# Two-block network on one core: late queries and U products moved between the spread batches, and the ranking of gathered heads moved by up to two dense steps

## What is computed

```
q = (hb @ w_q).reshape(C, PEER_HEADS, 2, PEER_DK_HALF)
s = einsum('thpd,hpnd->thpn', q, sub_keys)
sv, si = top_k(s, 16)
cand = sv[:, :, 0, :, None] + sv[:, :, 1, None, :]
fv, fpos = top_k(cand.reshape(C, PEER_HEADS, 256), 16)
g = softmax(fv)
a = gelu(einsum('ted,td->te', u_tab[eidx], hb))
y = einsum('te,ted->td', g * a, v_tab[eidx])
```

## Time and profile before

| | us |
|---|---|
| median of 3 runs (lowest, highest) | 2140.14 (2136.9, 2140.8) |
| the profiled execution's own time | 2128.76 |
| its span, first to last instruction | 2126.6 |
| TensorE busy | 2001.9 (94%) |
| VectorE busy | 1474.8 (69%) |
| GpSimd busy | 1064.6 (50%) |
| ScalarE busy | 454.8 (21%) |
| DMA bytes moved | 529.21 MB |

### The profile page before, as it was taken

One profiled execution on the slowest core, in us unless ns is written; L12 is line 12 of the kernel. 1 busy time (PEld: TensorE's weight loads), 2 busy tenths in 40 slices (PEclk: granted clock), 3 DMA queues, 4 the chain that ended last, 5 costly groups with the idle time before them and its releaser, 6 DMA issues.

```text
span 2126.6 us, 27946 instructions
## 1 busy us (share of the span) xinstructions
PE 2001.9 (94%) x10152; PEld 1490.0 (70%) x10152; DVE 1474.8 (69%) x3128; ACT 454.8 (21%) x916; POOL 1064.6 (50%) x905
## 2 busy tenths in 40 slices
PE   7999999999999998899988999999999999999796
PEld 6888866878898865678876666666666666666563
DVE  3673034333553596747997998989989898978668
ACT  4122223133453315522222010100101010010000
POOL 4354432427203743222534866675766757566562
PEclk9999999999999999999988999999999999999998
DMA  9565423524101312014447999999999999999996
GB/s 246 164 227 187 137 70 129 196 79 131 51 3 53 119 33 90 1 60 145 133 157 277 413 414 414 413 413 414 413 413 414 413 413 414 413 413 412 399 414 255
DMA packets 130070, 529.21 MB, mean 249 GB/s; under 512 B 14208, under 2 KB 18736, under 8 KB 113200
## 3 DMA queue, kind: packets, MB, share of 16 engines
q0 software_dynamic: 73728, 268.47, 31.8%
...
...
## 4 chain that ended last, share of the span: by engine, by line
PE 42%; DMA 29%; DVE 19%; POOL 4%; issue 4%; ACT 2%; SPq 0%; DVEq 0%; ACTq 0%; POOLq 0%
PE ps L782 26%; DMA work<-in_peer_v,consts 10%; DMA work<-in_peer_u,consts 7%; DMA ring<-in_peer_v,consts 6%; DMA ring<-in_peer_u,consts 6%; PE ps L1099 3%; PE ps L1111 2%; PE ps L868 2%; POOL ring L2377 1%; POOL work L2377 1%; PE ps L810 1%; PE ps L924 1%; DVE ring L1848 1%; DVE tables L1894 1%; DVE work L1894 1%
## 5 line engine op out<-in xcount | busy, mean ns | idle before, releaser
L1111 PE MATMUL ps<-work,tmp 128*128 128x512 f32 x1024 | 463.2, 606 | 22.9 <-DVE tmp L1914 22.9
L2298 POOL TENSOR_TENSOR w_lo<-ring,w_hi 128x1024 fp32r<-128x1024 f32 (+2 forms) x116 | 274.6, 2374 | 394.9 <-ACT w_hi L1969 394.8
L1099 PE MATMUL ps<-hT,work 128*128 128x256 f32 x2048 | 453.0, 379 | 0.0
L1099 PEld LDWEIGHTS ps<-hT,work 128*128 128x128 f32 x2048 | 388.8, 190 | 79.1 <-issue 29.6
L1111 PEld LDWEIGHTS ps<-work,tmp 128*128 128x128 f32 x1024 | 193.3, 193 | 246.3 <-issue 223.2
L2377 POOL DMA_INDIRECT ring<-in_peer_u,consts x136 | 174.1, 1280 | 118.2 <-DVE hT L1870 35.7
L2377 POOL DMA_INDIRECT ring<-in_peer_v,consts x138 | 165.4, 1199 | 104.1 <-DVE tables L1894 45.6
L782 PE MATMUL ps<-w_hi,x_hi 128*128 128x512 f32 (+2 forms) x544 | 208.2, 383 | 1.1 <-DVE tmp L1437 1.1
L782 PE MATMUL ps<-w_lo,x_hi 128*128 128x512 f32 (+2 forms) x544 | 207.2, 381 | 0.0
L1969 ACT ACTIVATE w_hi<-ring 128x1024 fp32r<-128x1024 f32 (+2 forms) x116 | 120.4, 1042 | 392.3 <-PE ps L782 287.2
L2377 POOL DMA_INDIRECT work<-in_peer_v,consts x118 | 149.6, 1268 | 84.9 <-DVE tables L1894 38.5
...
## 6 DMA issues: line engine op xcount, KB each, us to landing
work<-in_u_steps SPq DMA_DIRECT2D x64, 1024.0 KB, 8.0
work<-in_peer_v SPq DMA_DIRECT2D x64, 1024.0 KB
...
```

Of the source, the lines that this page charges most:

```text
L1099: mm = pe.matmul(ps[:, 4 + s, j * DT:(j + 1) * DT], u_ring[:, s, j, k, :], hT[:, k, GATHERED * P:T], start=(k == 0), stop=(k == KD - 1))
L1111: mm = pe.matmul(ps[:, 2 * t + half, :], tmp[:, s, j * DT + t * P:j * DT + (t + 1) * P], v_ring[:, s, j, half * BANK:(half + 1) * BANK], s ...
L2298: pool.tensor_tensor(w_lo[q % NPIECE][:, 0:n], ring[:, at:at + n], w_hi[q % NPIECE][:, 0:n], ALU.subtract).then_inc(w_split, 1)
```

## The change

Query 12 moves ahead of the spread batches: its first half between the second and the third transposed table, its second half behind the third. Queries 13 to 15 then fill batches m = 0 to 5, and the U products of dense steps 0 and 1 fill m = 6 to 13, a quarter of a step's product (one j, four of eight k) behind each batch. The third table moves to bank 1. In the ranking, the reduce (L1778) moves from piece 6 to piece 7, and the pieces of a head move: those of head 1 stand in dense steps 0 to 5, those of head 2 and later begin at s = 6 of the head before the last, so that piece 6 stands in s = 3, a U step, and piece 7 in s = 5.

```diff
--- before.py
+++ after.py
@@ -55,6 +55,8 @@
 BLOCK = SLOTS * 2 * GATHERED // STEPS
 HEAD_SLOTS = GATHERED * TOPK
 U_STEPS = HEAD_SLOTS // BLOCK
+FIRST_PIECES = ((0,), (1, 2), (3, 4), (5,), (6,), (7,))
+NEXT_PIECES = ((0,), (1,), (2, 3), (4,), (5,), (6,), (), (7,))
 EPS = 1e-6
 LAMBDA_INIT = 0.8 - 0.6
 NEG = -1.0e30
@@ -93,7 +95,7 @@
 ADA_LAG = 2
 ATT_LAG = 4
 LATE_FIRST = 12
-U_FIRST = 2 * (2 * PEER_H - LATE_FIRST)
+U_FIRST = 2 * (2 * PEER_H - LATE_FIRST - 1)
 ATT_SLOTS = 8
 C_CHUNKS = {0: Q_LAT, 1: KV_LAT + ROPE, 2: BANK, 3: BANK, 4: BANK}
 
@@ -232,11 +234,13 @@
         jobs.add("pqL", f)
         if f >= 1:
             jobs.add("peer_l", f - 1)
-    for i, b in enumerate((4, 5, 1)):
-        jobs.put(b, "pairs", i)
+    for i in range(2):
+        jobs.put(4 + i, "pairs", i)
     for f in range(LATE_FIRST, 2 * PEER_H + 1):
         if f < 2 * PEER_H:
             jobs.put(f % 2, "pqL", f)
+        if f == LATE_FIRST:
+            jobs.put((f + 1) % 2, "pairs", 2)
         jobs.put(2 + f % 2, "peer_l", f - 1)
     return jobs, units
 
@@ -1071,15 +1075,24 @@
                 if f >= 1:
                     key_scores("pqL", "peer_l", f - 1, f - 1)
 
-            pe.wait_ge(picked, 2 * PEER_H - 1)
-            for i in range(3):
-                pe.wait_ge(routed, 3 if i == 2 else 2)
+            def table(i, src):
+
                 o = start("pairs", i)
-                src = r_sel[:, i, :, :, :] if i < 2 else r_g
                 for t in range(DENSE):
                     mm = pe.transpose(o[:, t * P:(t + 1) * P],
                                       src[:, t, :, :].rearrange("p h k -> p (h k)"), ident[:])
                 end(mm, "pairs", i)
+
+            pe.sem_inc(spread_summed, 2)
+            pe.wait_ge(picked, 2 * PEER_H - 1)
+            pe.wait_ge(routed, 2)
+            for i in range(2):
+                table(i, r_sel[:, i, :, :, :])
+            query("pqL", "pql", LATE_FIRST, LATE, ALL[0:KD // 2])
+            pe.wait_ge(routed, 3)
+            table(2, r_g)
+            query("pqL", "pql", LATE_FIRST, LATE, ALL[KD // 2:])
+            key_scores("pqL", "peer_l", LATE_FIRST - 1, LATE_FIRST - 1)
 
             def spread_gates(m, s):
 
@@ -1091,14 +1104,14 @@
                                        hot_j[s][part][:, t // TWIN, :, t % TWIN], start=(part == 0), stop=(part == PARTS - 1))
                 mm.then_inc(spread_summed, 1)
 
-            def dense_u(s, load, js=range(PAIR)):
+            def dense_u(s, load, js=range(PAIR), ks=range(KD)):
 
                 pe.wait_ge(u_loaded[s], load)
                 for j in js:
-                    for k in range(KD):
+                    for k in ks:
                         mm = pe.matmul(ps[:, 4 + s, j * DT:(j + 1) * DT], u_ring[:, s, j, k, :],
                                        hT[:, k, GATHERED * P:T], start=(k == 0), stop=(k == KD - 1))
-                if js[-1] == PAIR - 1:
+                if js[-1] == PAIR - 1 and ks[-1] == KD - 1:
                     mm.then_inc(u_done, 1)
 
             def dense_v(n, s, load, first=False, last=False):
@@ -1117,19 +1130,18 @@
 
             for b in range(4, NB):
                 pe.wait_ge(bank_free[b], jobs.uses[b])
-            pe.sem_inc(spread_summed, 2)
             for m in range(RSTEPS):
                 spread_gates(m, m % 2)
-                f, half = LATE_FIRST + m // 2, m % 2
-                if f < 2 * PEER_H:
+                f, half = LATE_FIRST + 1 + m // 2, m % 2
+                if m < U_FIRST:
                     query("pqL", "pql", f, LATE, ALL[half * 4:half * 4 + 4])
                     if half == 1:
                         key_scores("pqL", "peer_l", f - 1, f - 1)
-                elif m < U_FIRST + 2 * PAIR:
+                elif m < U_FIRST + 4 * PAIR:
                     if m == U_FIRST:
                         key_scores("pqL", "peer_l", f - 1, f - 1)
-                    n, j = divmod(m - U_FIRST, PAIR)
-                    dense_u(n, 16, range(j, j + 1))
+                    n, j = divmod((m - U_FIRST) // 2, PAIR)
+                    dense_u(n, 16, range(j, j + 1), ALL[half * 4:half * 4 + 4])
             for b in range(4):
                 pe.wait_ge(bank_free[b], jobs.uses[b])
             for n in range(2):
@@ -1772,11 +1784,11 @@
                         eq = late[h].eq[a].rearrange("p (t k) a -> p t k a", k=TOPK)
                         late_steps(dve.tensor_tensor(eq, eq, r.idxf[:, a].unsqueeze(2).to_broadcast([P, n, TOPK, TOPK]),
                                                      ALU.mult))
+                else:
                     late_steps.settle()
                     for a in range(2):
                         eq = late[h].eq[a].rearrange("p (t k) a -> p t k a", k=TOPK)
                         late_steps(dve.tensor_reduce(late[h].sel[:, a], eq, AX.X, ALU.add))
-                else:
                     late_steps.settle()
                     late_steps(dve.scalar_tensor_tensor(eidx[:, h], late[h].sel[:, 0], float(NKEYS), late[h].sel[:, 1],
                                                         ALU.mult, ALU.add))
@@ -1916,10 +1928,12 @@
                     one_hots(region + 1, n + RSTEPS)
                 if s == U_STEPS:
                     head_coefs(h)
-                if h + 1 < PEER_H and s < 7:
-                    late_piece(h + 1, s)
-                    if s == 6:
-                        late_piece(h + 1, 7)
+                if n < len(FIRST_PIECES):
+                    for piece in FIRST_PIECES[n]:
+                        late_piece(1, piece)
+                elif (n + 2) // HEAD_STEPS + 1 < PEER_H:
+                    for piece in NEXT_PIECES[(n + 2) % HEAD_STEPS]:
+                        late_piece((n + 2) // HEAD_STEPS + 1, piece)
                 if s < U_STEPS:
                     gather_u(h, s)
                 else:
@@ -2195,7 +2209,7 @@
                 taken(act.activation(d_h2[:, i // 2, (i % 2) * BANK:(i % 2 + 1) * BANK], o, ACT.Copy), "h2", i)
             act.wait_ge(x_kept, 16 * NT)
             act.wait_ge(xn_done, NT * 4)
-            for f in range(LATE_FIRST):
+            for f in range(LATE_FIRST + 1):
                 if f == LATE_FIRST - 2:
                     normalise_gates()
                 keep_query("pqL", "peer_l", f)
@@ -2219,8 +2233,8 @@
             act.sem_inc(spread_kept, 2)
             for m in range(RSTEPS):
                 keep_gates(0, m)
-                f = LATE_FIRST + m // 2
-                if m % 2 == 1 and f < 2 * PEER_H:
+                f = LATE_FIRST + 1 + m // 2
+                if m % 2 == 1 and m < U_FIRST:
                     keep_query("pqL", "peer_l", f)
                     keep_late(f - 1)
                 if m == U_FIRST:
```

## The result

| | before | after |
|---|---|---|
| median, 5 runs each side by side | 2137.70 us | 2127.82 us |
| lowest to highest | 2135.91 to 2140.80 | 2123.18 to 2129.84 |
| profiled execution | 2128.76 | 2129.84 |
| its span | 2126.6 | 2128.0 |

The ratio of the times is 0.9948, with a 95% interval of 0.9930 to 0.9965: the changed kernel is faster by 0.35 to 0.70%, 7.5 to 15 us; the medians are 9.9 us apart. The forecast was 8.6 us less, 2131.5 us.

A forecast was written before the change was run, and what follows sets the result against it. The DMA stream was taken to bound the dense steps, its restart hanging on the spread batches' end. The loop's 8.6 us (4.1 plus 4.5), with ranking 0, off the 2140.1 us median gave 2131.5; own range 2129 to 2134, wider 2127 to 2137.5.

The forecast's parts named there:

- the saving is the same there: Whole kernel: the profiled execution's saving of 8.6 us also holds for the median of 2140.1 us, giving 2131.5.
- I take 0: Ranking pieces moved among the dense steps: no change in the end time, between -3 and +3 us.
- What bounds the kernel: Dense steps are bound by DMA at 413 GB/s; the spread batches' end sets the restart, and 8.6 us passes on whole.
- Query 12 moved ahead: Before batch 0: two halves of 1.82 us and 0.44 of scores fit TensorE's waits, cost nothing; the loop loses 4.1 us.
- The 4.5 left for the waits: Spread loop: VectorE's late-batch waits and the slow clock at batch 4 hold the remaining 4.5 us of the saving.
- Batches 0 to 5: Spread loop's start: VectorE stays last, first gather stays at 1102, 1.3 to 1.4 us lost at batch 4 is saved.
- Batches 6 to 15: Rest of the spread loop: 2.57 us a batch on TensorE, sixteenth batch kept near 1129.9 us, 8.6 us sooner.
- The profiled execution at 2120.2 us: Whole kernel: the profiled execution falls from 2128.8 us by 8.6 to 2120.2.
- rival (b): Dense steps: the ranking helps as well, the stream loses 2 to 3 us less, 2128 to 2129.5 us; 12%.
- Rival (c): Dense steps: slower, GpSimd's gather issue becomes the bound from 1.6 us an issue on, 14 us given back, 2145; 5%.
- Rival (d): Spread loop: half the gain, TensorE falls to the low clock again or batch 15 waits, 2134 to 2137 us; 10%.

The follow-up runs named there:

- a_again: The changed kernel run again unaltered on chip 0, beside the kernel before: ratio to before 0.9959, median 2125.97 us.
- spread_only: The changed kernel with the old ranking and the reduces of L1778 back in piece 6, on chip 0: ratio to the kernel before 0.9974, 2128.09 us.
- a_third: The changed kernel run once more unaltered on chip 11, beside the kernel before: ratio to before 0.9945, median 2126.70 us.
- s_third: The changed kernel with the ranking as before, on chip 11: ratio to the kernel before 0.9970, median 2131.48 us.
- early8: The changed kernel with all eight gathered rows of the first U step reduced before the wait for step 0's gelu, chip 11: ratio to before 0.9962, 2131.45 us.
- delay: The changed kernel with the U product of dense step 1 computed twice more behind batch 10, chip 15: ratio to the kernel before 1.0025, 2136.09 us.
- late_gathers: The changed kernel with the first gather held until the sixteenth batch's tables are written, chip 15: ratio to the kernel before 1.0004, 2131.71 us.
- rank_only: The kernel before with only the ranking pieces and the reduces of L1778 moved, chip 0: ratio to before 1.0002, median 2136.76 us.
- b_again: The kernel before run again unaltered on chip 0: ratio to before 1.0004, median 2136.54 us.

## Why the prediction was wrong, and what of it held

**Where the number went.** The median after, 2127.8 us, lies 3.7 under the forecast of 2131.5 and 1.2 under its own range, 2129 to 2134. Of the 3.7, 2.4 are the starting value: the three runs had a median of 2140.1, the five beside the changed kernel have 2137.7. The other 1.3 are the saving, 9.9 for 8.6, and the interval of 7.5 to 15 holds both. This much is no more than noise. The mechanism shows where the sum was wrong.

**The step that failed** is "the saving is the same there", together with the term for the ranking, "I take 0". Both took one profiled execution without a stall for the state of the kernel. Every trace of chips 0 and 11, of either kernel, has a stall in the loop, and there the ranking, taken as 0, comes out at 2.1 and 4.8 us by medians (a_again against spread_only, a_third against s_third; part of it is the 1 us of loop that the moved reduces give). The new order between the batches, without it, gives 7.2 and 6.6 us (spread_only, s_third; intervals 3 to 8 and 3 to 9), where the forecast has 8.6 for the whole loop. So that the saving of the pair came near the 8.6 may be luck in part: one term is too small, the other perhaps too large. Whether the five runs of the result had these stalls in the old ranking is not known: the trace of before shows none.

**What bounds the kernel** held. End less batch 15 is 988.1 to 989.2 us in the ten traces of the table that have neither large stalls in the dense steps nor changed gathers, over loops from 47.5 to 57.8 us. A loss in the middle of the stream, though, passes on only in part (3 of 8 us, above).

**Query 12 moved ahead** cost nothing where it went, as forecast: its second half and scores end at 1087.6, 2 us before batch 0 waits out. But it gives 2.4 us on top of the spread U and 2.7 to 2.9 alone, and the sum counted 4.1 for it. The 4.5 left for the waits were too small in turn: the spread U gives 4.5 to 4.7 and the moved reduces 1.1 to 1.6. The 8.6 stood because the two errors cancel.

**Batches 0 to 5.** Head 0's first gather is 19.1 us behind the start of the first tables in both traces, as forecast. The moved reduces shorten the wait before batch 4 and keep the query half behind it at full clock, as the prediction counted: 1.24 to 1.44 us and 1.97 in all ten traces that have them moved, 2.50 to 2.75 in the other eight, with a query half of 2.94 to 3.76 in seven of these. (The cost that it names, 3.27 - 1.82, is 1.45 us, not 1.3 to 1.4.) The clock behind the wait before batch 0: it was granted at 0.50 before, the 1.2 GHz level; now, after a wait of 1.97 us instead of 3.94, the first query half takes 2.94 us instead of 3.76, part of it at either level. The Trainium skill (TensorE: Matmul & The Clock Gate, Part 1) says that the clock follows how busy the engine has lately been; the traces agree, since that query half takes 1.97 us in eight of the twelve traces with query 12 moved ahead, 2.83 to 2.95 in four, and 3.76 in all six without. It was worth nothing in the end, since VectorE is last there: TensorE waits 1.44 and 1.16 us for the tables of batches 4 and 5.

**Batches 6 to 15.** 2.6 us a batch and the last one without a wait, as forecast (a_third and early8, after their stall, wait 0.67 and 0.25 us). The price, 43.8 us for the loop, was measured as 43.6 (delay), 43.9 (late_gathers) and 44.0 (after, less its stall).

**The profiled execution at 2120.2 us** was wrong: 2129.8. 4.4 us came from the start of the loop, and 5.6 from the stall. A stall on both sides leaves the difference between the loops as it is (7.3 to 9.1 us), and with it most of the forecast for the median.

**The ranking, "I take 0, between -3 and +3"**. On chip 15 no time shows it. On chips 0 and 11 the large stalls in the dense steps are in all three traces with the old ranking and in none of the five with the new one. The end is 2.6 to 5.6 us earlier without them (end less gather 15, 981.5 and 984.1 against 978.5 and 978.9). By medians it is 2.1 us on chip 0 and 4.8 on chip 11, but rank_only against b_again, on chip 0 too, shows nothing. So the traces show the effect, and the times do not yet prove it. That is rival (b), by a mechanism that the trace of before did not contain: its window of 1503 to 1747 us runs at 413 GB/s. For the pair of the result, whose interval is 7.5 to 15 us, its share stays unknown.

**Rival (c)**, GpSimd's issue as the bound, did not come. The groups of gathers, which answer to the earlier trace rows:

```profile
L2391 POOL DMA_INDIRECT ring<-in_peer_u,consts x136 | 178.7, 1314 | 130.4 <-DVE hT L1882 43.6
L2391 POOL DMA_INDIRECT ring<-in_peer_v,consts x138 | 176.4, 1278 | 83.7 <-issue 37.6
```

A V gather into these buffers went from 1.20 to 1.28 us (those into the others, named work, from 1.27 to 1.25), far from the 1.6 at which issue would decide. The slow form beside VectorE's reduce is there, 1.99 us at 1151.07, as the rule of the Trainium skill (GPSIMD Engine Reference, section Specifications) on the shared interface would have it, but for a few gathers a step.

**Rival (d)** is partly there: TensorE does fall to a lower clock in the new loop, for the one U part behind the stall.

**Open.** What causes the stall. No run takes the series of gathers away on a chip that stalls. A second explanation, that TensorE's instructions arrive late beside the gathers (the expectation of late_gathers names it), is as untested: both runs that hold the gathers back were on chip 15. So the stall is tied to chips 0 and 11 by the traces, and its cause is not shown. And rank_only on chip 0: its trace lacks the dense-step stalls and ends 978.6 us behind gather 15, 3.2 less than b_again's, and its loop is 0.9 us shorter, but its median is that of before (1.0002). One trace a kernel does not say how often the others stall.
